# Gathers of expert rows that alternate two by two instead of four by four, in a hybrid decoder step on one Trainium2 core

## What is computed

```python
def _peer(h, peer_wq, peer_sub_keys, peer_u, peer_v):
    ...
    experts = jnp.take_along_axis(cand_i, best_pos, axis=-1)      # n x 8 heads x 16
    g = jax.nn.softmax(best_s, axis=-1)
    act = jax.nn.gelu(jnp.einsum('nd,nhkd->nhk', h, peer_u[experts]).astype(jnp.float32))
    return jnp.einsum('nhk,nhkd->nd', (g * act).astype(peer_v.dtype), peer_v[experts])
```

## Time and profile before

| | us |
|---|---|
| median of 3 runs | 2990.62 (2988.86 to 2991.33) |
| span of the profiled execution | 2939.9 |
| median less that span | 50.7 |
| PE busy | 2089.1 (71%) |
| DVE busy | 1511.3 (51%) |
| POOL busy | 1484.4 (50%) |
| ACT busy | 602.4 (20%) |
| packets of the gathers' queue, share of 16 engines' span | 58.7% |

### The profile page before, as it was taken

One profiled execution on the slowest core, in us unless ns is written; L12 is line 12 of the kernel. 1 busy time (PEld: TensorE's weight loads), 2 busy tenths in 40 slices (PEclk: granted clock), 3 DMA queues, 4 the chain that ended last, 5 costly groups with the idle time before them and its releaser, 6 DMA issues. The chain is left out here.

```text
span 2939.9 us, 31629 instructions
## 1 busy us (share of the span) xinstructions
PE 2089.1 (71%) x10991; PEld 1320.7 (45%) x10991; DVE 1511.3 (51%) x3747; ACT 602.4 (20%) x1709; POOL 1484.4 (50%) x1509
## 2 busy tenths in 40 slices
PE   7999988986867877976779975764257676654044
PEld 6788854764655555643345452332134442111010
DVE  4421024056788986336641268778675665005820
ACT  4331036022323120004531112321011110000000
POOL 1210000024235576556644578767757676555775
PEclk9999989987988989988889986876678997778577
DMA  5223453445653889898879978989989999998998
GB/s 175 95 72 129 137 193 118 165 155 167 209 199 106 303 329 413 331 367 336 312 269 373 385 256 329 412 333 352 403 301 392 391 403 370 385 391 343 346 404 328
DMA packets 209781, 843.33 MB, mean 287 GB/s; under 512 B 25752, under 2 KB 32728, under 8 KB 190104
## 3 DMA queue, kind: packets, MB, share of 16 engines
q0 software_dynamic: 170912, 644.95, 58.7%
q1 hardware_dynamic: 38712, 196.36, 18.1%
HBM read 821.80 MB, written 23.54 MB: 288 GB/s over the span
## 5 line engine op out<-in xcount | busy, mean ns | idle before, releaser
L3282 POOL DMA_INDIRECT e_ring<-in_peer_u,e_idx x576 | 649.5, 1128 | 448.0 <-DVE e_dot L3438 206.4
L3282 POOL DMA_INDIRECT e_ring<-in_peer_v,e_idxT x576 | 617.2, 1072 | 338.8 <-issue 167.7
L3438 DVE CUSTOM_DVE_ANT_0 e_ring<-e_ring,e_h 128x1024 f32<-128x1024 f32 x576 | 703.4, 1252 | 148.0 <-DMA e_ring<-in_peer_u,e_idx 97.0
L3349 PE MATMUL ps<-e_ring,e_wz 128*32 128x512 f32 x2304 | 369.9, 773 | 372.3 <-DMA e_ring<-in_peer_v,e_idxT 368.3
L3349 PEld LDWEIGHTS ps<-e_ring,e_wz 128*32 128x32 f32 x2304 | 77.4, 128 | 581.2 <-issue 570.0
L360 PE MATMUL ps<-hTb,wb 128*128 128x320 f32 x384 | 110.1, 442 | 0.0
L1658 POOL CAST ra_atf<-ra_at 128x32 f32<-128x32 uint32 x8 | 1.7, 214 | 173.8 <-DVE ra_hit L1651 173.8
L360 PEld LDWEIGHTS ps<-hTb,wb 128*128 128x128 f32 x384 | 72.9, 195 | 28.7 <-issue 2.5
L3481 DVE TENSOR_TENSOR e_x<-e_x,ps 128x512 f32<-128x512 f32 x10 | 6.4, 683 | 153.8 <-PE ps L3349 153.8
L1057 POOL MEMSET inda<- 128x256 f32 x1 | 0.3, 312 | 161.4 <-POOLq L3729 161.4
L635 POOL TENSOR_TENSOR sa_xdt<-xnata,dt 128x512 f32<-128x512 f32 x8 | 8.3, 1043 | 114.1 <-POOLq L286 100.9
(11 more groups left out here) (730 smaller groups left out, 4301.4 us busy)
## 6 DMA issues: line engine op xcount, KB each, us to landing
wb<-in_weights SPq DMA_DIRECT2D x63, 1024.0 KB, 5.8
e_ring<-in_weights SPq DMA_DIRECT2D x36, 1024.0 KB, 4.8
wb<-in_late_weights SPq DMA_DIRECT2D x6, 2048.0 KB, 11.0
room<-in_late_weights SPq DMA_DIRECT2D x6, 2048.0 KB, 14.9
h<-in_weights SPq DMA_DIRECT2D x11, 1024.0 KB, 6.6
xs<-in_weights SPq DMA_DIRECT2D x10, 1024.0 KB, 7.6
e_ring<-in_peer_u,e_idx POOLq DMA_INDIRECT x576, 7.0
e_ring<-in_peer_v,e_idxT POOLq DMA_INDIRECT x576, 8.7
```

The lines of the kernel that those rows point to most:

```text
L3282: nc.gpsimd.indirect_dma_start(out=self.ring[:, self.slot(place), :], out_offset=None, in_=k.peer_u if kind == "u" else k.peer_v, in_offse ...
L3349: last = nc.tensor.matmul(k.ps[32 * b:32 * b + 32, self.SUMS + i, :], self.wz[:, at:at + 32], self.ring[:, self.slot(self.v_at[n]), 512 * ...
L3438: v.tensor_tensor_reduce(uu, uu, self.h[:, tile % 2, :], 1.0, 0.0, ALU.mult, ALU.add, self.dot[:, tile % 2, t:t + 1]).then_inc(self.dotted, 1)
```

## The change

`both` takes two u and two v in turn where it took four and four:

```diff
         def both(tu, a, b, tv, c):
-            for i in range(a, b, 4):
-                u(tu, i, i + 4)
-                v(tv, c + i - a, c + i - a + 4)
+            for i in range(a, b, 2):
+                u(tu, i, i + 2)
+                v(tv, c + i - a, c + i - a + 2)
```

## The result

The changed kernel takes 3025.23 us (median of 4 runs, 3020.06 to 3028.3), the kernel before on the same occasion 2989.74 us (4 runs, 2981.6 to 2991.33): ratio 1.0118, 95% interval 1.0096 to 1.0139. Forecast were 2997.3 us and 2986 to 3010. The direction was right, the size was not.

A forecast was written before the change was run, and what follows sets the result against it. It took PE's dense work, a PE-DVE-ACT chain and DMA to bound by stretches; 6.5 - 2.3 - 1.0 + 2.0 + 1.5 = +6.7 us gave a span of 2946.6, plus 50.7 the forecast 2997.3 us, range 2986 to 3010.

The forecast's parts named there:

- Term 4: DMA-bound stretches, 1802 to 2020 and 2142 to 2476: earlier sums and shorter v lookahead cost little, +2.0 and +1.5 us.
- Term 2: Group b's attention, 31 steps between L1498 rows: dots spread evenly save time, -2.3 us, ends -6 and +3.
- Term 1: End of group b's compressed attention: place 235's sum moves ahead of L1263, whose matmuls then follow PE's wait, +6.5 us.
- at most a doubling of the landing: Place 235's row, by the skill's rule: lands between 1309.0 and 1318.7; at the early end the forecast would be 2994 to 2997.
- Term 3: Stage "ba", PE-bound: one sum leaves it for the end of the attention, -1.0 us, ends -3.5 and 0.
- "nothing" for the rest of the range: First range, places 156 to 355: the other moved quads change places among dense matmuls without a wait, costing nothing.
- The offset of 50.7 us: Whole kernel: the median of the runs lies 50.7 us above the profiled span of 2939.9, added to reach the forecast.
- R1: DMA-bound stretches: nine places of lookahead are too few and gathers starve, 3018.4 us, with half the loss 3006.1; chance 0.14.
- R3: DMA-bound stretches: evenly spread dots end POOL's waits, DMA's share rises to 0.98, 2976.9 or 2983.5 us; chance 0.16.
- R2: No change: place 235 lands before 1305, or a later stage takes the loss up, 2990.8 us; chance 0.19.
- R4: POOL: paired dots lengthen each gather's issue by 0.05 us, +5.5 us, 3002.8 us; chance 0.05.
- The two signs for the whole: Forecast wrong if group b's attention begins no later, or if time from there to the end changes by over 8 us.

The follow-up runs named there:

- short ring: Kernel before, but in the second and third range POOL waits for a quad's sum two gathers sooner, lookahead 9 gathers instead of 11: 1.0064 of the kernel before.
- early sum: Kernel before with gathers and dots in their old order, each quad's sum in the second and third range two places sooner in PE's list: 1.0113.
- dots spread alone: Kernel before, but in places 156 to 355 the third and fourth dot of each four stand two places later in DVE's list: 0.9947 of the kernel before.
- batch 4: Follow-up runs that shift dots apart from gathers and sums; its copy of the unchanged kernel measured 0.9973, with a traced span of 2981.0 us.
- first range with late sum: Kernel before with pairs in places 156 to 355 alone, each quad's sum kept at its old place in PE's list: 0.9964 of the kernel before.
- batch 3: Follow-up runs; the two traces have pairs in the first range, alone (0.997) or with sums two places later in the second and third range (1.0006).
- gathers and sums only: Kernel before with gathers and sums in pairs in the first range, dots kept in fours on DVE: 1.0008 of the kernel before.
- spread dots: Kernel before with dots two by two on DVE in all three ranges, gathers and sums four by four: 1.0021 of the kernel before.
- batch 1: Follow-up runs with pairs in one range at a time; its copy of the unchanged kernel measured 1.0001, with a traced span of 2945.5 us.

## Why the prediction was wrong, step by step

**Term 4 failed, and with it the forecast.** It read "DMA's share is 0.95 and the transfers are the same; only what makes DMA run dry is lost", named both effects that do so, and sized them by what is free: +2.0 and +1.5 us. Ranges two and three measured 1.0095 and 1.0102, 47 us by the medians and 58 by the ratios. Its two effects are both real. The lookahead of nine places "fits, with 1.9 us to spare": the short ring alone costs 0.6%. "The dots stand behind updates that need PE's step, so they come later": sums two places sooner, with dots and gathers in their old order, cost 1.1%, and dots two places later cost 0.7%. The fault was to treat a share of 0.95 as a reserve that absorbs delays. It went with the old rhythm: in the sample attention it is 0.93 to 0.97 in the unchanged kernel's traces, 0.91 and 0.88 in the changed kernel's. I also took PE's waits as harmless where DMA bounds; by the chain above they are so only as long as nothing that feeds DMA stands behind them, and here dots do. The early sum shows that moving them costs time; the way from there to the gathers is read from the waits and was not tested link by link.

**Term 2 had the right sign and an eighth to a fifth of the size.** Forecast -2.3 us with ends -6 and +3; dots spread alone make the stage 11.0 us shorter (batch 4) and, across batches of like total, 18.7. The sign that was named for it, L1498 rows over 176 to 178 us, was not met as it stands: they span 181.2 us in the changed kernel, where the faster execution of before had 179.3 and the unchanged one of batch 4 191.5. Steps grouped by the number of dots in them showed little bend, and I took that to be the price of a dot. But such a grouping sees only the step a dot stands in; what a crowded step delays in the steps behind it is charged to those. That reason is argued; the size is measured.

**Term 1 was right in its mechanism.** PE waits 19.63 us at L3349 ahead of L1263 in the changed kernel, and the compressed stage grew from 38.9 to 44.8 us: +5.9 for a forecast of +6.5. Some of that is not the moved sum: with pairs but L1263 ahead of the wait again (first range with late sum) the stage took 40.7. Nor does the wait hold in every execution: it was 2.14 and 3.69 us in two traces of batch 3, where the stage took 36.2. The rows:

```profile
1335.33 3.64 PE L3349 MATMUL ps<-e_ring,e_wz 128*32 128x512 f32 x16 [19.63 <-DMA e_ring<-in_peer_v,e_idxT]
1338.90 4.48 PE L1263 MATMUL ps<-cpb_pT,zs 128*128 128x256 f32 x16
...
1345.92 0.92 PE L1406 MATMUL ps<-ksT,qTb 64*128 64x384 f32 x4 [2.55 <-PEq L1174]
```

A rule of the Trainium skill, in "DMA: Bandwidth & Descriptors", section on queues, rings and completion order, says that each engine takes packets from its queues in turn, and I had estimated from it that the row would land early. The taking of turns fits the trace: from 1310 to 1320 in the kernel before the gathers' queue (q0) and SP's (q1), which carries the large transfer, share the engines nearly evenly (packets, MB, share of 16 engines):

```profile
q0 software_dynamic: 485, 1.78, 49.4%
q1 hardware_dynamic: 32, 2.06, 47.7%
```

What failed is my estimate of at most a doubling of the landing. The waits of 14.96 us in the earlier trace rows, 19.63 and 21.62 at this sum speak against it, those of 2.14 and 3.69 us fit it. Why the row comes with the end of the transfer in most traces and early in two is open.

**Term 3 and "nothing" for the rest of the range failed.** "Ba" was to win 1.0 us and lost 7.6, in the changed kernel, and 8.9 with gathers and sums only. The other moved quads were costed at nothing, "without a wait", and the turn of the tile's weights was not costed at all; the waits of 4.1 (the turn), 1.5 and 1.1 us above are new. And the way to the attention lost 11.7 us in all, not 5.9: 3.3 in the branch stage and 2.5 in the keys, values and queries besides. One place is the start of the queries' stage, where a sum now stands first. PE's matmuls of the stage before end 5.26 us ahead of it, while the meeting of the engines is late:

```profile
1245.85 3.64 PE L3349 MATMUL ps<-e_ring,e_wz 128*32 128x512 f32 x16 [5.26 <-PEq L1033]
```

The five other traces with this order have 1.14 to 5.24 us there, the kernel before 0.88. What makes that meeting late is open.

**The offset of 50.7 us** was no part of the kernel, as told above. It did no harm here, since the ratio is what was wrong.

**The rivals.** R1, with 0.14, came nearest in time (3018.4); its mechanism, tested alone, carries about a third of the loss of the two ranges, and in the changed kernel POOL waits only 5.3 us for sums. The share of DMA in the state stages, 0.90, is below the 0.92 that was to speak for it; but the early sum and the spread dots, which leave the lookahead alone, lower the share in the sample attention to 0.87 and 0.88, so the share does not tell R1 from the chain through the dots. R3 had "faster, by the even spread of dots" in the wrong stretches: the spread is worth its gain where a chain bounds, and in the DMA-bound ones it costs 0.7%. R2 is excluded by the interval. The two signs for the whole: the attention did begin later, but from there to the end the changed kernel took 31.6 us more than the unchanged one of batch 4, where 8 was the bound. R4 does not show: gathers of v and u in the sample attention take 1188 and 1028 ns in the changed kernel and 1268 and 999 in the unchanged one of batch 4.

## What to carry to other kernels

Do not cost a wait at nothing because its engine does not bound: follow its list to what stands behind it, down to the next producer of free slots. A DMA share of 0.95 is no cushion: 0.6% of the time went when the gathers could run ahead nine places instead of eleven. Look for everything that hangs on a place that you move; here the steps that close a tile went along unseen. Ask of each stage which engine comes last to its end: here a transfer of 4032 KB came within 2.5 us of PE. Where one edit changes several lists at once, write them out as separate tables (here sums and dots) before measuring: one half of this change is worth having, and the whole hid it.

## What the runs showed of the hardware

The unchanged kernel's median moved between 2937 and 2989 us from batch to batch, several times what one batch resolves; 2938.9 and 2977.3 were measured on the same chip. Stages do not scale alike: group b's attention took 197.4 us in one trace and 207.5 in another of the same kernel, at granted clocks of 0.84 and 0.83 (the unchanged kernel of batch 1, then of batch 4):

```profile
1339.00:1536.00 197.00, 144.97 (x865) 67.53 (x861) 130.81 (x254) 96.01 (x229) 123.87 (x111) 0.84 0.85 302
```

```profile
1337.00:1544.00 207.00, 148.94 (x864) 69.42 (x861) 129.09 (x251) 96.38 (x229) 118.98 (x110) 0.83 0.81 284
```

A row gathered behind a transfer of 4032 KB was waited for between 2.14 and 21.62 us at one and the same sum. The transfer itself and the stores around it had landed 26.6 to 30.1 us after its issue in all twenty traces, with the gathers' queue moving about as many bytes beside it.
